# Two passes instead of three in the down product of experts with up to 64 rows

## The reference, cut to what matters

```
hu  = xblk @ w_up[e] + b_up[e]                     # 1024 -> 2048
g   = minimum(hu[:, 0::2], 7);  u = clip(hu[:, 1::2], -7, 7)
act = (u + 1) * g * sigmoid(1.702 * g)             # 1024
y   = act @ w_down[e] + b_down[e]                  # 1024 -> 1024
out[token] += gate * y
```

## Time and profile before

| | |
|---|---|
| median of 3 runs | 1750.04 us (1747.75 to 1750.27) |
| the profiled execution: its own time | 1752.75 us |
| its span, first to last instruction | 1751.1 us |
| busy: PE, DVE, ACT | 1496.4, 1288.8, 1000.4 us |
| the experts' stage | some 521 to 1694 us of the span |

### The profile page before, as it was taken

How to read it: one execution, slowest core, us unless ns; L and a number is a source line. 1 busy time by engine, 2 the same in 40 slices (tenths; PEclk the granted TensorE clock), 3 DMA queues, 4 the chain that set the end, 5 groups by cost and what they waited for, 6 DMA issues and landing times.

```text
span 1751.1 us, 22646 instructions
## 1 busy us (share of the span) xinstructions
PE 1496.4 (85%) x6955; PEld 1155.0 (66%) x6956; DVE 1288.8 (74%) x1315; ACT 1000.4 (57%) x865; POOL 304.8 (17%) x416
## 2 busy tenths in 40 slices
PE   5982878859987899999999999999999999999850
PEld 3761667633536677777877777777887778778740
DVE  0337553763426899999889999999977997898836
ACT  0011332510105788888668878878756886787620
POOL 5304888600120000100100010000000001000000
PEclk8996775759887999999999999999988999999975
DMA  9985352321317899999979999999967999799732
GB/s 353 350 244 145 91 215 97 88 91 51 136 49 268 335 380 387 388 386 388 357 286 387 385 391 379 388 385 390 386 243 285 382 391 360 272 397 385 268 140 82
DMA packets 123834, 498.26 MB, mean 285 GB/s; under 512 B 20945, under 2 KB 46114, under 8 KB 89522
## 3 DMA queue, kind: packets, MB, share of 16 engines
q1 hardware_dynamic: 103026, 454.30, 68.5%
q0 software_dynamic: 14768, 29.16, 4.9%
q10 hardware_dynamic: 5984, 14.11, 2.3%
HBM read 499.17 MB, written 26.25 MB: 300 GB/s over the span
## 4 chain that ended last, share of the span: by engine, by line
PE 54%; DVE 17%; issue 12%; ACT 7%; SPq 5%; DMA 3%; DVEq 1%; ACTq 0%; POOL 0%; POOLq 0%
PE psum L533 51%; DVE w_lo L1660 8%; ACT w_hi L1152 5%; SPq L390 4%; PE psum L536 3%; DMA arena<-in_w_up 1%; DMA early<-in_pages 1%; DVE arena L1716 1%; DVE arena L1785 1%; DVE arena L1335 1%; DVE arena L1208 1%; DVE arena L1336 1%; DVE arena L1237 1%; SPq L387 0%; ACT arena L1029 0%
## 5 line engine op out<-in xcount | busy, mean ns | idle before, releaser
L1660 DVE TENSOR_TENSOR w_lo<-arena,w_hi 128x2048 fp32r<-128x2048 f32 x384 | 860.7, 2285 | 63.6 <-ACT w_hi L1152 51.1
L1152 ACT ACTIVATE w_hi<-arena 128x2048 fp32r<-128x2048 f32 x376 | 715.2, 1917 | 237.3 <-PE psum L533 236.9
L533 PE MATMUL psum<-w_hi,x_split 128*128 128x512 f32 x2208 | 581.9, 398 | 18.0 <-DVE x_split L1672 9.5
L533 PEld LDWEIGHTS psum<-w_hi,x_split 128*128 128x128 f32 x2208 | 417.5, 191 | 105.4 <-issue 18.7
L533 PE MATMUL psum<-w_lo,x_split 128*128 128x512 f32 x1536 | 433.8, 405 | 49.0 <-DVE w_lo L1660 44.2
L533 PE MATMUL psum<-arena 128*128 128x64 f32 (+11 forms) x2270 | 424.4, 365 | 52.2 <-DMA arena<-in_w_in 18.7
L533 PEld LDWEIGHTS psum<-arena 128*128 128x128 f32 (+5 forms) x2270 | 334.3, 217 | 144.2 <-issue 82.5
L533 PEld LDWEIGHTS psum<-w_lo,x_split 128*128 128x128 f32 x1536 | 282.8, 191 | 154.8 <-DVE w_lo L1660 100.8
L1856 POOL DMA_INDIRECT y_dram<-y_part,arena x32 | 49.6, 1551 | 1046.4 <-ACT y_part L1135 954.7
L536 PE MATMUL psum<-arena 128*128 128x128 f32 (+4 forms) x501 | 81.9, 318 | 77.3 <-ACT arena L1035 30.3
L536 PEld LDWEIGHTS psum<-arena 128*128 128x128 f32 (+4 forms) x501 | 67.1, 160 | 93.9 <-issue 60.6
(11 more groups left out here) (204 smaller groups left out, 758.0 us busy)
## 6 DMA issues: line engine op xcount, KB each, us to landing
arena<-in_w_up SPq DMA_DIRECT2D x256, 1024.0 KB, 7.5
arena<-in_w_down SPq DMA_DIRECT2D x128, 1024.0 KB, 6.9
early<-in_pages SPq DMA_DIRECT2D x160, 128.0 KB, 2.8
arena<-in_w_in ACTq DMA_DIRECT2D x23, 512.0 KB, 7.3
arena<-in_pages POOLq DMA_DIRECT2D x32, 128.0 KB, 7.6
early<-in_pages POOLq DMA_DIRECT2D x32, 128.0 KB, 6.5
arena<-in_pages SPq DMA_DIRECT2D x32, 128.0 KB, 2.2
early<-in_w_plg SPq DMA_DIRECT2D x1, 4096.0 KB, 14.3
```

Source lines behind the costliest of these rows:

```text
L533: return TE.matmul(out, lhsT, rhs, start=start, stop=stop, skip_group_check=True)
L1152: SE.activation(w_hi[:, (8 + t) % 3], chunk_in[(8 + t) % 6], ACT.Copy).then_inc(hi_ready, 1)
L1660: VE.tensor_tensor(w_lo[:, at], chunk_in[buf], w_hi[:, at].bitcast(f32), SUB).then_inc(lo_ready, 1)
```

## The change

For few items the down product gets the form of the up product: `act_lo` is written into columns 64 to 127 of the tile `act_hi`, and PE makes two passes (with `w_hi`, with `w_lo`), 32 matmuls instead of 48. Rows 64 to 127 of the PSUM result are copied by ACT to a tile `y_low` on rows 0 to 63, and DVE adds them to PSUM rows 0 to 63 into `y_rows` (`result_sum`), behind part 2 of the next item and ahead of its hidden rows. DVE then tells POOL and PE that the result is there. ACT's sigmoid and copy to `act_hi` do half the columns for few items.

For many items the three passes stay. Their second half is turned into banks 4 and 5 instead of 6 and 7, for which PE waits until the result of i-1 is out of them, no longer for DVE's reading of the first half. Their result is copied in two instructions.

`set_turner` and the tile `turner` go; a fixed tile `folder` takes their place. On DVE part 10 now stands ahead of the low part of the rows of i+2, no longer behind it. PE's down product, and ACT's result copy, sigmoid and `hidden_high`, stand in branches now. Ahead of the first item DVE clears two more tiles (`act_sb`, and rows 64 to 127 of `y_rows`).

```diff
             def turn_hidden(i, many_slots, x_next, begin):
                 pe.wait_ge(hu_ready, i * 4 + 4)
-                pe.wait_ge(turner_ready, i + 1)
                 pe.wait_ge(xlo_ready, x_next)
                 with pe.If(many_slots > 0):
-                    turn_half(turner, 1)
-                    pe.wait_ge(turned_read, i * 2 + 1)
-                    turn_half(ident[:, HALF:CAP], 1)
+                    turn_half(ident[:, 0:HALF], 6).then_inc(hu_turned, 1)
+                    if not begin:
+                        pe.wait_ge(y_ready, i)
+                    turn_half(ident[:, HALF:CAP], 4).then_inc(hu_turned, 1)
                 with pe.If(many_slots < 1):
-                    turn_half(turner, 2)
+                    turn_half(folder, 6).then_inc(hu_turned, 2)
...
+                with pe.If(many_slots > 0):
+                    product(((act_hi, w_hi), (act_lo, w_hi), (act_hi, w_lo)))
+                with pe.If(many_slots < 1):
+                    product(((act_hi, w_hi), (act_hi, w_lo)))
...
+            def result_copy(i, used, many_slots):
+                with act.If(many_slots > 0):
...
+                    SE.activation(y_rows[:, 0:512], psum[:, 4, :], ACT.Copy).then_inc(y_half, 1)
+                    SE.activation(y_rows[:, 512:D], psum[:, 5, :], ACT.Copy).then_inc(y_ready, 1)
+                with act.If(many_slots < 1):
...
+                    SE.activation(y_low.rearrange("p (c n) -> p c n", c=2), psum[HALF:CAP, 4:6, :], ACT.Copy).then_inc(y_half, 1)
...
+                    SE.activation(act_sb[:, :, 0:HALF], gg[:, :, 0:HALF], ACT.Sigmoid, scale=SALPHA).then_inc(e_ready, 1)
...
+                    SE.activation(act_hi[:, :, 0:HALF], act_sb[:, :, 0:HALF], ACT.Copy).then_inc(act_hi_ready, 1)
...
             VE.memset(gg, 0.0)
+            VE.memset(act_sb, 0.0)
+            dve.wait_ge(rows_out, 16 * 13)
+            VE.memset(y_rows[HALF:CAP], 0.0)
             VE.memset(act_lo.bitcast(f32), 0.0)
...
+                    VE.tensor_tensor(act_hi[:, :, HALF:], act_sb[:, :, 0:HALF], act_hi[:, :, 0:HALF].bitcast(f32), SUB).then_inc(act_lo_ready, 1)
+
+            def result_sum(i, many_slots):
+                with dve.If(many_slots < 1):
+                    dve.wait_ge(y_half, i + 1)
+                    VE.tensor_tensor(y_rows[0:HALF].rearrange("p (c n) -> p c n", c=2), psum[0:HALF, 4:6, :],
+                                     y_low.rearrange("p (c n) -> p c n", c=2), ADD).then_inc(y_ready, 1)
...
                 for t in range(3):
                     part(t)
+                if not begin:
+                    result_sum(i - 1, is_many(i - 1))
                 hidden_rows(i, e, here)
...
-                for t in range(5, 8):
-                    part(t)
-                set_turner(i + 1)
-                part(8)
-                part(9)
+                for t in range(5, 11):
+                    part(t)
                 if end < NE - 1:
                     rows_low(i + 2, is_many(i + 2))
-                part(10)
                 part(11)
```

More of the change, by code:

```diff
@@ L292, in build @@
         stats2, mv2, rstd2 = ec.take(2, 6), ec.take(2), ec.take(1)
-        turner, turn_fold, few, many_f = ec.take(HALF), ec.take(HALF), ec.take(NI + 8), ec.take(NI + 8)
+        folder, many_f = ec.take(HALF), ec.take(NI + 8)
         GTs = ec.take(NT)
@@ L926, in up_product, with down_product, product @@
                     product(((x_hi, w_hi), (x_hi, w_lo)))
-            def down_product(i, s, first):
+            def down_product(i, s, first, many_slots):
                 pe.wait_ge(act_hi_ready, i + 1)
                 pe.wait_ge(act_lo_ready, i + 1)
[L931 to L940, removed]
+                def product(passes):
+                    for q in range(4):
+                        at = (first + q) % 3
+                        pe.wait_ge(hi_ready, s + (q + 1))
+                        for n_pass, (x, w) in enumerate(passes):
+                            if w is w_lo:
+                                pe.wait_ge(lo_ready, s + (q + 1))
+                            for a, c in ((0, 0), (0, 1), (1, 0), (1, 1)):
+                                last = mm(psum[0:CAP, 4 + c, :], x[:, 2 * q + a], w[:, at, a * D + c * 512:a * D + c * 512 + 512],
+                                          q == 0 and n_pass == 0 and a == 0, q == 3 and n_pass == len(passes) - 1 and a == 1)
+                        last.then_inc(chunk_used, 1)
+                with pe.If(many_slots > 0):
+                    product(((act_hi, w_hi), (act_lo, w_hi), (act_hi, w_lo)))
+                with pe.If(many_slots < 1):
+                    product(((act_hi, w_hi), (act_hi, w_lo)))
             def is_many(i):
@@ new lines, in squash, with hidden_high @@
+            def squash(i, many_slots):
+                with act.If(many_slots > 0):
+                    act.wait_ge(g_ready, i + 1)
+                    SE.activation(act_sb, gg, ACT.Sigmoid, scale=SALPHA).then_inc(e_ready, 1)
+                with act.If(many_slots < 1):
+                    act.wait_ge(g_ready, i + 1)
+                    SE.activation(act_sb[:, :, 0:HALF], gg[:, :, 0:HALF], ACT.Sigmoid, scale=SALPHA).then_inc(e_ready, 1)
+            def hidden_high(i, many_slots):
+                with act.If(many_slots > 0):
+                    act.wait_ge(act_ready, i + 1)
+                    SE.activation(act_hi, act_sb, ACT.Copy).then_inc(act_hi_ready, 1)
+                with act.If(many_slots < 1):
+                    act.wait_ge(act_ready, i + 1)
+                    SE.activation(act_hi[:, :, 0:HALF], act_sb[:, :, 0:HALF], ACT.Copy).then_inc(act_hi_ready, 1)
@@ L1672, in rows_low @@
                     VE.tensor_tensor(x_hi[:, :, HALF:], turned[:, :, 0:HALF], x_hi[:, :, 0:HALF].bitcast(f32), SUB).then_inc(xlo_ready, 1)
-            def set_turner(i):
-                VE.scalar_tensor_tensor(out=turner, in0=turn_fold, scalar=few[:, bass.ds(i, 1)], in1=ident[:, 0:HALF], op0=MUL, op1=ADD)\
-                    .then_inc(turner_ready, 1)
             LINKS = 5
@@ L1682, in hidden_rows, with half @@
                 bias = bup[:, bass.ds(e, 1)].rearrange("p a (s j) -> p (a s) j", s=2)
-                sums = [psum[:, 6 + s, :].rearrange("p (j n) -> p j n", j=8) for s in range(2)]
-                def half(cols, turned, bank_read, g_done, weight, at):
+                def half(cols, at_bank, turned, bank_read, g_done, weight, at):
                     dve.wait_ge(hu_turned, i * 2 + turned)
+                    sums = [psum[:, at_bank + s, :].rearrange("p (j n) -> p j n", j=8) for s in range(2)]
                     g, u = gg[:, :, cols], uu[:, :, cols]
@@ L1739, in item @@
                     part(3)
+                    result_sum(i, here)
                     return
```

81 lines of the change are left out of this document (39 added, 42 removed).

## The result

The changed kernel takes 1736.9 us (median of 6 runs, 1734.85 to 1744.7), the kernel before 1749.49 in the same session (6 runs, 1747.75 to 1750.27). The ratio is 0.9946, with a 95% interval of 0.992 to 0.9971: faster, by 12.6 us or half a percent, where 27.7 us were forecast. The profiled execution took 1734.85 us, with a span of 1733.2: 17.9 less than the span of before. PE is busy for 65 us less (1431.0 against 1496.4), which is more than the whole gain.

What follows compares the result with a forecast made beforehand. The prediction took a few item to be bound by the order of work in a ring through PE, ACT and DVE, with no engine standing out. Its terms summed to -27.7 us, giving 1722 us, range 1712 to 1738.

Steps and rivals of the forecast that it cites:

- 18 few items between few items: DVE's waits shrink, so each item takes 0.6 us less; -9.0 us taken for all.
- 3 few items behind many ones: Old down product and no sum, only the 0.2 us wait at part 5 goes: -0.6 us.
- 4 pairs: A few item, then a many one: second half turned earlier, still at half clock; -3.0 us each, -12.0 us.
- item 22: Many item behind a many one: idle between turned halves goes, second half at full clock; -6.0 us.
- start: Two more memsets on the path to the first `w_hi`: +1.9 us.
- end: Last down product has fewer matmuls, ACT's work is halved, a branch and the sum are added: -2.0 us.
- The failed step: Few items: PE's new idle of 0.7, 0.9 and 1.6 us at the chunks' `w_lo` costs nothing.
- rival 3: PE's idle lowers the clock ahead of few items' turning: 4.4 us an item, 1762 us with half hit; chance 0.05.
- the layout: Few item's timeline on DVE, ACT and PE, laid out anew with the change: 32.6 us an item.
- The clean few item: Few item between few items: 32.6 us from scatter to scatter, DVE's sum 1.2 us behind part 2.
- Rival 1: Loads become the bound at 389 GB/s, few items stay at 33.2 us: 1735 us, chance 0.22.
- rivals 2, 3 and 4: Sum not taken up, 1740 us, chance 0.08; clock falls in few items, 1762, 0.05; more gain than forecast, 1706, 0.10.

Runs made afterwards that it cites:

- e5: Changed kernel plus one spare matmul behind the down product of all few items but the last: 1719.18 us, ratio 0.9823.
- e11: Changed kernel with two more loads of the same register ahead of each turning: 1836.96 us, ratio 1.0509.
- e3: Kernel before with one edit, DVE's part 10 put ahead of the low rows of i+2: 1743.05 us, ratio 0.9983.
- e4: Changed kernel with part 10 put back behind the low rows: 1752.83 us, ratio 1.0025.
- e7: Changed kernel with the sum made over only 64 of the 1024 columns: 1723.21 us, ratio 0.986.
- e6: Changed kernel plus one spare matmul behind few items' down product and three between the turned halves of many items: 1704.67 us, ratio 0.9772.
- e8: Changed kernel with three passes in few items' down product too, everything else kept: 1743.24 us, ratio 0.9949.
- e1: Changed kernel plus four spare matmuls ahead of the `w_lo` pass of parts 10 and 11 of few items: 1731.34 us, ratio 0.9916.
- e10: Kernel before plus three spare matmuls between the turned halves of items over 64 rows: 1734.34 us, ratio 0.9909.

## Why the prediction was wrong

By its terms, in the profiled executions (spans, -17.9):

| | forecast | measured |
|---|---|---|
| 18 few items between few items | -9.0 | -0.8 |
| 3 few items behind many ones | -0.6 | -0.6 |
| 4 pairs | -12.0 | -9.8 |
| item 22 | -6.0 | -6.0 |
| start | +1.9 | +2.3 |
| end | -2.0 | -3.0 |

- **The failed step** is the sentence "PE's new idle (0.7, 0.9 and 1.6 us at the chunks' `w_lo`) costs nothing", and with it the 0.05 for rival 3. The term that rests on it, -9.0 for 18 few items, measured -0.8. PE's new idle costs time by way of the clock: not by the waits for `w_lo` alone, of which the trace has 0.58 and 0.69 us, but together with 0.57 us ahead of the turning that the sentence doesn't list. In the first profile four few items had half clock and took 34.4 to 36.0 us; had they taken 32.7 like their neighbours, that would be 8.8 us less (1.9 + 3.3 + 1.7 + 1.9), and the 18 items would have come to -9.6. Shown by e5, where that is so (the 21 items without half clock, and the 18 items of the forecast at -9.9 against before), and by e11, where more idle brings it in every item.
- **What the layout did not have** is the idle that decides. It followed waits between engines, and PE's sequencer is none of them. In the changed kernel 1.77 us go by from the start of the last four matmuls (973.97), for which PE waited on `w_lo` of part 11, to the turning (975.74). The sequencer's loop end, register load and branches lie in between, and four matmuls, 0.9 us, are all the cover they have. In the kernel before the turning starts right behind the down product, for more matmuls are queued there. The prediction asked this of ACT's branches and not of PE's.
- **Rival 3 named the mechanism** and the place. Its price, 4.4 us an item, is near e11's 4.9; in the first profile of the changed kernel an item loses 1.7 to 3.3, since a part of the turning still runs at the upper clock (6.52 us, against 7.08 in e11). Its chance was too low: what spoke against it, "the long idle is now between full-width matmuls", looked at the wrong idle. The Trainium skill ("TensorE: Matmul & The Clock Gate", "HAM oscillation — how this bites in real kernels") tells of a kernel whose bursts of matmuls are parted by DMA waits of about 3 to 5 us and start at the lower clock each time. The trace agrees in kind but not in size: here the clock fell behind idle of 0.66 us ahead of the last four matmuls and 0.54 ahead of the turning.
- **The clean few item** was right: 32.72 against 32.6, wait for wait on DVE, and the sum at 1.13. So were its two conditions: the swap counts only with the shorter product (e3, e4), and the shorter product is worth 0.68 an item (33.40 - 32.72), not the 3.7 that PE is spared.
- **Rival 1 is out**: at 32.7 us and 393 GB/s one `w_hi` in all items waits for a load, for 0.28 us, and at 32.0 us in e7 (396 GB/s in its window) none does. That the measured 1736.9 lies inside the stated range, next to rival 1's 1735, is luck: the range was drawn as far as that for the loads. It left out rivals 2, 3 and 4, whose chances add to 0.23 and not to some 0.17.
- **Pairs**: two of the four gave -3.5 against -3.0. The other two gave -2.1 and -0.7, with 17 us and 10 us at half clock where the first two have 7: most likely the same cause, in a place where the forecast had half clock once and no more. In e6, without any, the pairs take 76.2 to 77.6. The forecast also took one pair of before (82.1) for all four, which are 80.9 to 84.4.
- **Item 22** was right in its size and its cause: e8 has the gain (40.28) with three passes, so it belongs to the second half's banks.
- **Start and end**: +2.3 against +1.9 is luck, since the start differs by 15 us from one execution to another, and the end was -3.0 against -2.0.
- **The median**: the rest, from 17.9 to 12.6, is that the profiled execution of after lies 2.05 below its median and that of before 3.26 above. The prediction took only the second part, at 2.7, and left no margin for how much executions differ.

## What to carry to other kernels

When an engine is relieved, ask what its new idle does to the clock, and read the idle directly ahead of the densest work, the sequencer's "issue" included: a wait moved closer to a loop's end uncovers register loads and branches that had cost nothing. PE that isn't the bound was worth keeping busy here: one spare matmul an item, and three in some, gave 18 to 26 us from the experts' start on (1157.5 and 1165.2 to 1139.0), and the change itself 12 to 20 (from 1177.7). But idle is not dear in itself: e4's longer wait brought half clock into the down product, where DVE was the bound, and cost next to nothing. Before crediting a change with a gain, try the filler on the old kernel.

## What the runs showed of the hardware

- PE's clock fell to its lower level ahead of or in the turning of few items at "issue" idle of 0.52 to 0.58 us behind two waits for `w_lo` of 0.45 to 0.7 (1.2 for the second in an item ahead of a many one), in 4 and in 6 of 21 like places (the changed kernel); with 1.8 to 1.9 us of "issue" idle, in all 21 (e11); with "issue" idle alone, of 0.52 and 0.78 us in the two hit, in 2 (e1); where only the waits of 0.57 and 0.69 for `w_lo` were left, in none (e5).
- A wait of 1.79 to 2.11 us between the turned halves brought the lower level in all five items over 64 rows of the kernel before; filled with three spare matmuls, in none (e10).
- Adding two loads of a register on PE's sequencer added 1.27 us of idle in front of the matmuls behind them.
- The stretch ahead of the experts took from 562 to 577 us in the profiled executions, with 212 to 253 us of it at the lower clock, least where it was short. No run here explains why.
